# Waiting tile by tile at two stage starts, an earlier load order, and scaled copies on ScalarE in place of products on GpSimd

## The reference

```python
# first block: hybrid mixer (8 heads of attention + gated linear recurrence), then a product-key expert layer
h = _rmsnorm(x, g_mix) * (1 + sc1) + sh1;  x = x + ga1 * _hybrid_mixer(h, ...)
h = _rmsnorm(x, g_ffn) * (1 + sc2) + sh2;  x = x + ga2 * _peer(h, ...)
x = _rmsnorm(x, g_final)
# second block, layer 0: a diagonal complex state space over 128 groups of 16 channels and 64 states
u, z = split(h @ w_in)
bu_re = einsum('blgc,gnc->blgn', ug, bb_re);  bu_im = ... bb_im
x_re, x_im = scan of x[t] = a * x[t-1] + bu[t]      # a = mag * exp(i * theta), per group and state
y = einsum('blgn,gcn->blgc', x_re, c_re) - einsum(x_im, c_im) + d_skip * u
y = gelu(y); y = y * sigmoid(y @ w_glu + b_glu); out = (y * silu(z)) @ w_out
```

## Time and profile before

| | us |
|---|---|
| median of 3 runs (3587.88 to 3587.96) | 3587.92 |
| the profiled execution | 3590.77 |
| its span in the trace | 3589.1 |
| PE busy | 3398.9 (95%) |
| DVE busy | 2489.4 (69%) |
| ACT busy | 1373.3 (38%) |
| POOL busy | 388.2 (11%) |

### The profile page before, as it was taken

One profiled execution on the slowest core, in us unless ns is written; L12 is line 12 of the kernel. 1 busy time (PEld: TensorE's weight loads), 2 busy tenths in 40 slices (PEclk: granted clock), 3 DMA queues, 4 the chain that ended last, 5 costly groups with the idle time before them and its releaser, 6 DMA issues. The chain is left out here.

```text
span 3589.1 us, 56839 instructions
## 1 busy us (share of the span) xinstructions
PE 3398.9 (95%) x20884; PEld 3069.1 (86%) x20884; DVE 2489.4 (69%) x4546; ACT 1373.3 (38%) x1996; POOL 388.2 (11%) x401
## 2 busy tenths in 40 slices
PE   3899998999999999999999999899989899999998
PEld 2688887889877999999999998788789898999998
DVE  7666556868387777777777776888867634666665
ACT  1333311013244444444444444322244434555553
POOL 0010120000000000000000000688810000000000
PEclk8999999999999999999999999999999999999999
DMA  9678744446777888888888886122247643555543
GB/s 402 274 298 305 274 165 141 147 157 233 283 279 292 293 293 293 294 296 295 296 296 295 294 294 246 59 94 102 105 179 270 240 141 130 190 185 188 188 167 139
DMA packets 123318, 817.74 MB, mean 228 GB/s; under 512 B 12848, under 2 KB 18224, under 8 KB 27184
## 3 DMA queue, kind: packets, MB, share of 16 engines
q1 hardware_dynamic: 105696, 761.31, 58.0%
q10 hardware_dynamic: 17488, 54.58, 4.0%
HBM read 791.65 MB, written 24.18 MB: 227 GB/s over the span
## 5 line engine op out<-in xcount | busy, mean ns | idle before, releaser
L532 PE MATMUL bank<-H,ring 128*128 128x256 f32 x3680 | 821.1, 382 | 30.8 <-PEq L377 13.4
L532 PEld LDWEIGHTS bank<-H,ring 128*128 128x128 f32 x3680 | 701.5, 192 | 127.5 <-issue 25.6
L1845 DVE TENSOR_TENSOR vlo<-ring,vhi 128x1024 fp32r<-128x1024 f32 x448 | 547.5, 1225 | 289.4 <-ACT vhi L1247 287.8
L1247 ACT ACTIVATE vhi<-ring 128x1024 fp32r<-128x1024 f32 x448 | 474.0, 1060 | 607.0 <-PE bank L602 317.0
L1531 DVE TENSOR_TENSOR wlo<-ring,whi 128x1024 fp32r<-128x1024 f32 x272 | 331.9, 1231 | 324.9 <-ACT whi L1060 321.6
L568 PE MATMUL bank<-Hhi,whi 128*128 128x256 f32 x1920 | 485.7, 290 | 22.6 <-DVE Hlo L1542 10.1
L569 PE MATMUL bank<-Hlo,whi 128*128 128x256 f32 x1920 | 476.1, 285 | 0.0
L1060 ACT ACTIVATE whi<-ring 128x1024 fp32r<-128x1024 f32 x272 | 287.3, 1059 | 360.8 <-PE bank L573 322.6
L595 PE MATMUL bank<-vhi,Ghi 128*128 128x512 f32 x1024 | 402.7, 393 | 13.5 <-ACT vhi L1247 13.5
L596 PE MATMUL bank<-vhi,Glo 128*128 128x512 f32 x1024 | 401.6, 392 | 0.0
L568 PEld LDWEIGHTS bank<-Hhi,whi 128*128 128x128 f32 x1920 | 370.6, 193 | 33.0 <-issue 18.0
(11 more groups left out here) (430 smaller groups left out, 4553.4 us busy)
## 6 DMA issues: line engine op xcount, KB each, us to landing
ring<-in_peer_u SPq DMA_DIRECT2D x128, 1024.0 KB, 5.2
ring<-in_peer_v SPq DMA_DIRECT2D x128, 1024.0 KB, 5.0
arena<-in_w_mod SPq DMA_DIRECT2D x96, 1024.0 KB, 6.9
ring<-in_w_ada SPq DMA_DIRECT2D x72, 1024.0 KB, 7.4
ring<-in_w_qz SPq DMA_DIRECT2D x64, 1024.0 KB, 4.8
ring<-in_w_in SPq DMA_DIRECT2D x35, 1024.0 KB, 7.1
ring<-in_ssm_in SPq DMA_DIRECT2D x32, 1024.0 KB, 5.0
ring<-in_w_mod SPq DMA_DIRECT2D x32, 1024.0 KB, 5.7
```

What stands on the lines that cost most here:

```text
L532: last = mm(out, ring[:, pos % R, k, :], rhs[:, k, :], start=(k == 0), stop=(k == KT - 1))
L1247: A(vhi[:, half], v_half(pos, half), ACT.Copy).then_inc(s("vhi_ready"), 1)
L1845: v.tensor_tensor(vlo[:, half], v_half(pos, half), vhi[:, half].bitcast(F32), ALU.subtract)\
```

## The change

1. SP, head 0: the order becomes skip 0, skip 1, load 2, skip 3, skip 4, load 5, load (1,0), the three `head_beside`, load 7, load (1,1), skip 6; the wait for `f_in_psum` goes. DVE does `whole_vec` of position 5 before `vectors` in head 0.
2. Top-k: the first GEMM waits for each tile of `H` by itself.
3. State space, start: PE signals the barrier and goes on into the first u GEMM, tile by tile; it waits for the barrier after that GEMM. ACT does `u_out(0, 0)` before the two tables. POOL clears `Cst` and builds the first masks before the barrier. DVE scales one tile of `x` after j = 3 of each tile in place of 16 at the start.
4. State space, loop: `masks` goes from POOL to ACT, behind the second `table` of the next tile and ahead of Silu, as 16 copies of 64 columns and 4 copies of 4x16 columns, each with a column of `in16`, `in64` or `neg64` as its scale.

```diff
 SP
-            for pos in range(8):
-                if pos in FIRST:
-                    head_skip(pos)
-                else:
-                    head_load(0, pos)
-            sp.wait_ge(s("f_in_psum"), 1)
+            for pos in (0, 1):
+                head_skip(pos)
+            head_load(0, 2)
+            for pos in (3, 4):
+                head_skip(pos)
+            head_load(0, 5)
+            head_load(1, 0)
             for n in range(3):
                 head_beside(0, n)
+            head_load(0, 7)
+            head_load(1, 1)
+            head_skip(6)
...
 PE
+                        if rows is not None:
+                            pe.wait_ge(s("biased"), rows + k + 1)
                         last = mm(out, ring[:, pos % R, k, :], rhs[:, k, :], start=(k == 0), stop=(k == KT - 1))
...
-            pe.wait_ge(s("biased"), 2 * KT)
...
-                    gemm("topk", i, 3 * h, banks[0][:, 0:T], 0, uses[0] + n)
+                    gemm("topk", i, 3 * h, banks[0][:, 0:T], 0, uses[0] + n, rows=KT if h == 0 else None)
...
-            pe.wait_ge(s("biased"), 3 * KT)
-
-            meet(pe, met)
+
+            pe.drain().then_inc(stage_end, 1)
+            met[0] += 4
...
-            u_half(0, 0, 0)
-            u_half(0, 0, 1)
+            u_half(0, 0, 0, 2 * KT)
+            u_half(0, 0, 1, 2 * KT)
+            pe.wait_ge(stage_end, met[0])
             b_times_u(0, 0, 0)
...
 ACT
+            def masks(i, t):
+
+                tile = 2 * i + t
+                act.wait_ge(s("y_pair"), 4 * tile + 1)
+                for ri in range(2):
+                    for n in range(8):
+                        A(Bst[:, t % 2, ri, n:n + 1, :], BB[:, ri, bass.ds(tile, 1), :], ACT.Copy, scale=in16[:, n:n + 1])
+                for ri in range(2):
+                    diagonal = Cst[:, t % 2, ri].rearrange("p (j c) -> p j c", j=4)
+                    for n in range(2):
+                        A(diagonal[:, :, 16 * n:16 * n + 16], CC[:, ri, bass.ds(4 * tile, 4), :], ACT.Copy,
+                          scale=(in64, neg64)[ri][:, n:n + 1])
+                act.drain().then_inc(s("masks_built"), 1)
...
                     table(1, (t + 1) % 2, 2 * tile + 3, None if first else 4 * tile + 4)
+                    masks(i, t + 1)
                 product(act, "ssm", i, 2 * t + 1)
...
+            u_out(0, 0)
             for duo in range(2):
                 table(duo, 0, duo, None)
-            u_out(0, 0)
...
 DVE
+                whole_vec("heads", i, 5, 33 + 3 * i)
                 if first:
                     vectors(i)
-                whole_vec("heads", i, 5, 33 + 3 * i)
...
+                    if j == 3:
+                        xk = x[:, bass.ds(tile, 1), :]
+                        v.scalar_tensor_tensor(xk, xk, V("g_final")[:, bass.ds(tile, 1)], rstd1, ALU.mult, ALU.mult)
...
-            for k in range(KT):
-                v.scalar_tensor_tensor(x[:, k, :], x[:, k, :], V("g_final")[:, k:k + 1], rstd1, ALU.mult, ALU.mult)
...
 POOL
-                    if j == 0 and not last:
-                        masks(i, t + 1)
-
+
+            pool.wait_ge(s("y_done"), 1)
             gp.memset(Cst_all, 0.0)
+            pool.wait_ge(s("disc_loaded"), 32)
             pool.drain()
             masks(0, 0)
+            meet(pool, met)
```

More of the change, by code:

```diff
@@ L455, in _, with rest_of_head @@
             sp.dma_start(gate_w, a["gate_w"][0]).then_inc(s("gatew_loaded"), 16)
-            for pos in range(8):
-                if pos in FIRST:
-                    head_skip(pos)
-                else:
-                    head_load(0, pos)
-            sp.wait_ge(s("f_in_psum"), 1)
+            for pos in (0, 1):
[5 more added lines that the diff above has]
+            head_load(1, 0)
             for n in range(3):
                 head_beside(0, n)
-            with sp.Fori(1, HEADS) as i:
-                for pos in range(2):
-                    head_load(i, pos)
+            head_load(0, 7)
+            head_load(1, 1)
+            head_skip(6)
+            def rest_of_head(i):
                 sp.wait_ge(s("gates_in_psum"), i + 1)
@@ L472, in _ @@
                         head_beside(i, pos // 2 - 1)
+            rest_of_head(1)
+            with sp.Fori(2, HEADS) as i:
+                for pos in range(2):
+                    head_load(i, pos)
+                rest_of_head(i)
             with sp.Fori(0, 2) as i:
@@ L522, in _, with gemm @@
             uses = [0, 0, 0, 0]
-            def gemm(stage, i, pos, out, bank, need=None, rhs=H, halves=(0, 1)):
+            def gemm(stage, i, pos, out, bank, need=None, rhs=H, halves=(0, 1), rows=None):
                 if need is not None:
@@ L848, in _, with u_half @@
             final_sums()
-            pe.wait_ge(s("biased"), 3 * KT)
-            meet(pe, met)
+            pe.drain().then_inc(stage_end, 1)
+            met[0] += 4
             pe.sem_inc(s("bu_read"), 2)
-            def u_half(i, t, half):
+            def u_half(i, t, half, rows=None):
                 b = 2 * t % 4
-                gemm("ssm", i, 2 * t, banks[b][:, 0:T], b, uses[b] + i + t // 2 if half == 0 else None, halves=(half,))
+                gemm("ssm", i, 2 * t, banks[b][:, 0:T], b, uses[b] + i + t // 2 if half == 0 else None, halves=(half,), rows=rows)
             def z_half(i, t, half):
@@ L2280, in _ @@
             pool.sem_inc(s("y_read"), 2)
-            meet(pool, met)
             def masks(i, t):
```

## The result

| | before | after |
|---|---|---|
| median, us | 3587.90 (3586.68 to 3587.96, 4 runs) | 3703.64 (3701.65 to 3705.93, 4 runs) |
| profiled execution's span, us | 3589.1 | 3699.9 |
| mean granted clock | 0.981 | 0.965 |

The ratio is 1.032, 95% interval [1.0305, 1.0334]: slower by 115.7 us. The prediction was 3678 (3642 to 3716).

The account below looks back on a forecast made before the run. A state-space loop of waits through PE, DVE and ACT was to bind: 26.7 us plus 2.1 for the clock, 28.8 a tile. State space +100, top-k -6, first head -4 made +90: 3678 us, range 3642 to 3716.

Parts of the forecast that it names:

- The first part of the loop: State-space tile: PE from b(t,0) through c3, for which `y_out` of tile t-1 waits; 12.3 us.
- The clock term: State-space loop: PE's clock falls after its wait ahead of b(t+1,0), adding 2.1 us to each tile.
- DVE from `y_out` to the end of the fraction: State-space loop: DVE from `y_out` through j = 2 to the end of `fraction`; 7.1 us.
- 20 copies: ACT's mask copies in the state-space loop: 0.24 us each, 4.8 a tile; ends 3.4 and 7.4.
- State space together: Whole state-space stage, its start, loop and last tile summed: +100 us.
- Start of the state space: PE begins at 2252.2 instead of 2258.67; b(0,0) at 2262.5 and b(1,0) at 2289.8.
- First head: PE's 4.12 us wait for a ring load after head 0 goes; load (1,3) lands about 156; gain 4 us.
- POOL relieved: State-space loop: moving masks off POOL gives DVE back at most 0.24 us a tile, 3.6 in all; counted as nothing.
- Scalings of x in the loop: State space: 0.42 us a tile returns after j = 3, covered by DVE's wait for b(t+1,0); uncovered 6.3 us.
- that the clock holds: Rival: the state-space loop is there but PE keeps 2.4 GHz, 29 us less, 3649; chance 0.12.
- copies take 0.37: Rival: ACT's state-space copies are slower, or tables reload each tile, 39 us more, 3717; chance 0.16.
- faster after all: Rival: ACT runs a tile ahead, so the state space falls to PE's 20.7 us a tile, 3560; chance 0.04.

Follow-up runs that it names:

- e6: Changed kernel with the loop's masks back on POOL after j = 0 and the 16 x scalings back at the stage start: 3577.80 us, ratio 0.997.
- e5: e2 with the 16 scalings of x back at the start of the state space: 3589.26 us, ratio 0.9999.
- e2: Changed kernel with ACT's 20 copies moved between `u_out` and table 1: 3615.37 us, ratio 1.0074.
- e4: Changed kernel plus twelve filler matmuls of ones on PE before it waits for the next tile's matrices: 3664.06 us, ratio 1.0208.
- e11: Kernel before with only the first head's edits (SP load order, DVE's vector 5 first): 3586.4 us, ratio 0.9988.
- e10: Changed kernel with the 16 input copies first in ACT's tile, the other 4 last, x scalings at stage start, old fraction: 3588.78 us, ratio 0.9996.
- e8: Changed kernel with DVE's fraction rewritten so no instruction has two SBUF inputs: 3688.61 us, ratio 1.0281.
- e12: e6 with each fraction's first product made by ACT as two scaled copies, Silu of z one tile back: 3559.87 us, ratio 0.9915.
- e1: Changed kernel with the loop's masks back on POOL after j = 0: 3599.26 us, ratio 1.0029.
- e7: e2 with the fraction rewritten without two-SBUF-input instructions and the x scalings after the last tile: 3584.74 us, ratio 0.9993.

## Why the prediction was right, and where it was off

Right in direction and mechanism, 26 us short in size. The chain e6, e5, e2, after splits the loss, each step one edit (us from the ratios times 3590; in all 115, as measured):

| step | edit added | us |
|---|---|---|
| before to e6 | the starts alone (head and top-k 9, state space the rest) | -11 |
| e6 to e5 | matrices from POOL to ACT, off the loop | +10 |
| e5 to e2 | scalings of x into the loop | +27 |
| e2 to after | copies behind table 1: the loop and its clock | +88 |

By the prediction's own steps:

- *The first part of the loop.* b(t,0) to `y_out`: 12.3 and 2.1 for the clock predicted, 15.15 measured (2368.86 to 2384.01). The first 12.3 stand: e4, which takes the clock's share away, is 2.8 a tile faster. The clock term was mis-sized by 0.7. I had taken it from the excess of first GEMMs after other stalls.
- *DVE from `y_out` to the end of the fraction*: 7.1 predicted, 7.87 measured. This is the other mis-sized term. The row that I read had the product at 0.93; here it is 1.71. With 14 tiles the two terms are 10 and 11 us of the 26.
- *Table 1*: 2.1 predicted, 2.08 measured. *20 copies*: 4.8 predicted, 4.87 measured; 16 take 3.93, 0.245 each, against the 0.24 that I took. The computed addresses cost nothing. The rows gave 0.21, and the step from there to 0.24 came from no row. The Trainium skill's price ("ScalarE: Activation LUTs", What ACT_TABLE_LOAD costs), from which the estimate of 0.24 had come, agrees. The start after a drain is 0.28, not 0.16, and copies to PE 0.27, not 0.2: together 3 us.
- *Tile*: 28.8 predicted, 30.5 measured, 24 us over 14 tiles. *State space together*: +100 predicted, +125.1 measured (PE's last work ahead of it is 10.4 us earlier, the last `y_out` 114.7 later).
- *Start of the state space*: L543 at 2242 predicted, 2241.99 measured; b(0,0) at 2252.5 and 2252.69; first tile 27.3 and 26.1. *Last tile*: 26.4 and 26.9.
- *Top-k start*: 6 earlier predicted, 6.2 measured.
- *First head*: 4 predicted, 2.6 in the change's trace, 2.2 in e11's. Load (1,3) did come at 156, and PE was 4 us earlier there (156.05 against 160.05). What came after was left out: PE runs on the low clock for longer behind its 2.72 us wait (8.58 against 7.17 for 32 records), and is at 171.51 against 174.10.
- *POOL relieved*: "I count nothing". That was the failed step. I had read the 0.93 as a collision and reasoned that less work on POOL can only lessen it. It did the opposite. In the kernel before the matrices keep POOL late: DVE's product after j = 0 starts ahead of POOL's, and the one after j = 2 meets only POOL's short sums. In the change POOL waits for `z_ready`, which is given just ahead of the next DVE product, and starts 0.1 to 0.2 us before it in every steady tile. e10 less e6 prices it at 9 to 11 us off the loop; in the loop the product's 0.78 a tile is 11 us, and e8, which also gets some clock back, gains 15. Off the loop (e5, e10) DVE keeps the first place after j = 0, by 0.2 to 0.3 us; no run shows what decides that.
- *Scalings of x in the loop*: predicted to come back at 0.42 a tile, under the wait for b(t+1,0). In the change that cover holds: the 1.38 us lie in a wait (DVE idles 4.1 after it). With the cover gone I had said 6.3 us for 15 tiles; e5 against e2 says 27. The same collision, with POOL's first product of j = 3; and with the scaling in the loop the fraction after j = 0 falls behind POOL as well (1.68 in e2, 0.69 in e5).

The rivals: that the clock holds is refuted by the windows and e4, that copies take 0.37 by 0.245. The "faster after all" rival wanted 3560 from tiles of 20.7 us. e12 reaches both numbers, but by relieving DVE; no place of the copies on ACT gave less than 3584, since with the matrices off POOL either the collision or the longer fraction that avoids it leaves DVE fuller than it was.

What stays open: from the last `y_out` to the end of the span the change's trace is 3.9 us shorter than that of the kernel before (966.6 against 970.5), e1 to e10 and e12 1.6 to 3.2, e11 0.6. Each is a single execution, and ten executions of one kernel here lie up to 10 us apart, so whether this is a gain is not shown.

## What to carry to other kernels

Before work is moved to an idle engine, write down what stands ahead of it in that engine's order and what waits behind it; if the chain comes back to its own start, its length is the new time of the loop, however idle the engine is. Behind table 1 the copies cost 88 us more than ahead of it. Then ask which lag the moved work had given: here the two engines collided when one started on the other's signal. And find the full engine first: here it was DVE, which the change did not relieve, and 1.6 us a tile taken from it were worth 18 us (e6 to e12).

## What the runs showed of the hardware

- A DVE instruction of fp32 with both inputs in SBUF and a POOL product that start within 0.1 to 0.2 us of each other hold each other up: 128x512 took 1.67 to 1.71 us against 0.69, 128x256 with a third, per-partition operand 1.38 against 0.42; whichever is second takes longer (e10's rows). With one SBUF input and one in PSUM, or one SBUF input and a per-partition operand, nothing was lost (0.87 for two of 256 columns in e7 and e8). The Trainium skill ("SBUF — State Buffer", Who interferes with whom) says that a DVE instruction with two SBUF inputs contends with GpSimd instructions that read SBUF, and that issue order decides who blocks; the traces agree.
- PE idle for 7 us came back at 1.2 GHz and stayed there for some 5 us of work; 24 records of filler ahead of the wait kept it at 2.4 GHz through a gap of 1.6 us (e4).
